# The first block's expert gather turned round: tokens stationary, in f32, with a ninth piece of weights loaded ahead

## What is computed

```python
def expert_choice_ffn(h, w_router, w_gate, w_up, w_down):
    cap = 2 * S // 16                                   # 64 tokens for each of 16 experts
    aff = softmax(h @ w_router)
    gate, idx = top_k(aff.transpose(0, 2, 1), cap)      # each expert chooses its tokens
    xe = h[idx]                                         # the gather: 16 x 64 x 1024
    hid = silu(xe @ w_gate) * (xe @ w_up)               # each weight 1024 x 1024
    ye = (hid @ w_down) * gate
    return zeros.at[idx].add(ye)                        # the scatter
```

## Time and profile before

| | us |
|---|---|
| median of 3 runs | 2611.15 (2604.75 to 2613.42) |
| the profiled execution, its own time | 2608.86 |
| its span in the profile | 2607.0 |
| mean granted TensorE clock | 0.973 of 2.4 GHz |
| PE busy | 2362.6 (91%) |
| DVE busy | 1134.7 (44%) |
| ACT busy | 911.7 (35%) |
| POOL busy | 241.9 (9%) |
| DMA, mean rate over the span | 250 GB/s |

### The profile page before, as it was taken

How to read it: one execution, slowest core, us unless ns; L and a number is a source line. 1 busy time by engine, 2 the same in 40 slices (tenths; PEclk the granted TensorE clock), 3 DMA queues, 4 the chain that set the end, 5 groups by cost and what they waited for, 6 DMA issues and landing times. The chain is left out here.

```text
span 2607.0 us, 31029 instructions
## 1 busy us (share of the span) xinstructions
PE 2362.6 (91%) x12565; PEld 1482.3 (57%) x12565; DVE 1134.7 (44%) x1678; ACT 911.7 (35%) x1228; POOL 241.9 (9%) x114
## 2 busy tenths in 40 slices
PE   6999799888887999799888888999999899989997
PEld 5735533333335835543333328887788777767776
DVE  4984312111214984321112125656612112458997
ACT  3256211111114256211111116656622234247775
POOL 0000100000000000100000005000244322200000
PEclk8999899999998989899999999999999999989999
DMA  9702499999999503399999995423123421149995
GB/s 347 277 1 100 159 388 409 410 410 410 410 408 356 211 0 119 153 409 409 410 410 409 410 405 166 162 81 97 65 85 89 133 76 54 49 159 379 369 372 215
DMA packets 276595, 650.47 MB, mean 250 GB/s; under 512 B 12144, under 2 KB 110718, under 8 KB 276222
## 3 DMA queue, kind: packets, MB, share of 16 engines
q1 hardware_dynamic: 272756, 637.98, 65.1%
q0 software_dynamic: 2592, 7.87, 0.8%
q10 hardware_dynamic: 1130, 2.99, 0.3%
HBM read 641.99 MB, written 8.39 MB: 249 GB/s over the span
## 5 line engine op out<-in xcount | busy, mean ns | idle before, releaser
L837 PE MATMUL ps<-ring,hy 128*64 128x512 f32 x992 | 225.6, 596 | 49.7 <-DMA ring<-in_w_up 32.2
L837 PE MATMUL ps<-ring,scr 128*64 128x512 f32 x992 | 225.2, 596 | 37.3 <-DMA ring<-in_w_up 31.3
L1343 DVE TENSOR_TENSOR scr<-scr,ps 128x512 f32<-128x512 f32 x32 | 22.0, 687 | 541.2 <-PE ps L837 541.2
L864 PE MATMUL ps<-ring,scr 128*64 128x512 f32 x1024 | 227.2, 595 | 4.1 <-ACT scr L1054 2.7
L1609 POOL TENSOR_TENSOR raw_r<-raw,w_high 128x2048 fp32r<-128x2048 f32 (+1 forms) x38 | 164.6, 4342 | 463.5 <-ACT w_high L1876 463.5
L1631 PE MATMUL ps<-x_high,w_high 128*128 128x512 f32 x464 | 187.4, 404 | 7.3 <-DVE y L2272 7.3
L2752 DVE TENSOR_TENSOR ring_r<-ring,ring_high 128x2048 fp32r<-128x2048 f32 x77 | 173.0, 2285 | 28.3 <-ACT ring_high L2629 28.2
L1633 PE MATMUL ps<-x_high,raw_r 128*128 128x512 f32 x464 | 184.5, 398 | 0.0
L837 PEld LDWEIGHTS ps<-ring,hy 128*64 128x64 f32 x992 | 69.2, 137 | 202.3 <-issue 122.4
L1632 PE MATMUL ps<-xT_r,w_high 128*128 128x512 f32 x464 | 183.5, 396 | 0.0
L837 PEld LDWEIGHTS ps<-ring,scr 128*64 128x64 f32 x992 | 68.1, 137 | 188.4 <-issue 121.1
(11 more groups left out here) (581 smaller groups left out, 4520.4 us busy)
## 6 DMA issues: line engine op xcount, KB each, us to landing
ring<-in_w_up SPq DMA_DIRECT2D x64, 2048.0 KB, 23.6
ring<-in_w_down SPq DMA_DIRECT2D x64, 2048.0 KB, 23.5
ring<-in_w_gate SPq DMA_DIRECT2D x60, 2048.0 KB, 23.3
ring<-in_w_up SPq DMA_DIRECT2D x56, 1024.0 KB, 6.9
ring<-in_w_ada SPq DMA_DIRECT2D x22, 2048.0 KB, 13.7
ring<-in_w_down SPq DMA_DIRECT2D x28, 1024.0 KB, 6.6
raw<-in_w_in SPq DMA_DIRECT2D x24, 1024.0 KB, 5.0
raw<-in_w_in SPq DMA_DIRECT2D x20, 512.0 KB, 5.2
```

The costliest lines, as they stand in the source:

```text
L837: mm = pe.matmul(ps[CAP * half:CAP * (half + 1), 1 + j // 2, :], x_e[j % 2][:, at_x:at_x + CAP], weights[:, k, half * HALF:(half + 1) * HA ...
L864: mm = pe.matmul(ps[CAP * half:CAP * (half + 1), 4, :], hidT[:, at_f:at_f + CAP], weights[:, k, half * HALF:(half + 1) * HALF], start=(j = ...
```

## The change

`gather` is turned round: `h_tok` in f32 is the stationary side, in blocks of 128 tokens by 128 channels, and s_pair, now f32, is the moving side with 128 columns. For each of 8 tiles of channels, 4 products add up; the result already stands as channels by slots in PSUM, where DVE's `tokens` reads it. So the eviction to `x_rows`, `turn_tokens`, ACT's rounded copies (line 1039) and POOL's subtractions (line 501) go. The first half of `one_hot_T`, which held the high part, takes (1, 2) as a third early piece, issued with (1, 0). The slots of the ring move by one: the six loads that wait for pieces 1 to 6 are now (1, 3) to (2, 2), and the rule 6e + j - 5 holds from (2, 3) on. Three loads for the next layer (`load_ada`) wait for one more used piece each.

```diff
-    early = [... for x, a in ((hy, CHUNK), (one_hot_T, CHUNK))]
+    early = [... for x, a in ((hy, CHUNK), (one_hot_T, CHUNK), (one_hot_T, 0))]
...
-        slot = (j - 3) % 6
+        slot = (j - 1 - EARLY) % 6
...
-            for e, j in ((0, 0), (0, 4), (0, 5), (1, 0)):
+            for e, j in ((0, 0), (0, 4), (0, 5), (1, 0), (1, 2)):
                 load(e, j)
             for n in range(6):
                 sp.wait_ge(chunk_used, n + 1)
                 load(1 + (n + EARLY) // 6, (n + EARLY) % 6)
...
-                    sp.wait_ge(chunk_used, used - (5 - c))
+                    sp.wait_ge(chunk_used, used - (4 - c))
                     load_ada(sp, A, M, after, c, ahead)
-                sp.wait_ge(xe_mm, 2 * PAIRS)
+                sp.wait_ge(xeT_mm, 2 * PAIRS)
...
-            for i in range(2 * TT):
-                pool.wait_ge(htok_ev, i + 1)
-                cs = slice((i % 2) * HALF, (i % 2 + 1) * HALF)
-                pool.tensor_tensor(h_low3[:, i // 2, cs], h_tok3[:, i // 2, cs], h_high3[:, i // 2, cs].bitcast(F32), ALU.subtract).then_inc(htok_low, 1)
...
             def gather(n):
                 pe.wait_ge(s_built, n + 1)
                 for half in range(2):
-                    cs = slice(half * HALF, (half + 1) * HALF)
-                    for t in range(TT):
-                        pe.matmul(ps[:, GATHER_BANKS[half], :], s_pair[:, t, :], h_high3[:, t, cs], start=(t == 0), stop=False)
-                        mm = pe.matmul(ps[:, GATHER_BANKS[half], :], s_pair[:, t, :], h_low3[:, t, cs], start=False, stop=(t == TT - 1))
-                    mm.then_inc(xe_mm, 1)
-            def turn_tokens(n):
-                for half in range(2):
-                    pe.wait_ge(xe_kept, 2 * n + (half + 1))
                     for b in range(4):
                         kt = 4 * half + b
-                        mm = pe.transpose(ps[:, GATHER_BANKS[half], b * P:(b + 1) * P], x_rows[:, kt * P:(kt + 1) * P], ident)
+                        for t in range(TT):
+                            mm = pe.matmul(ps[:, GATHER_BANKS[half], b * P:(b + 1) * P], h_tok3[:, t, kt * P:(kt + 1) * P], s_pair[:, t, :], start=(t == 0), stop=(t == TT - 1))
                     mm.then_inc(xeT_mm, 1)
...
                     gates(n + 1)
-                    turn_tokens(n + 1)
...
-                act.activation(h_tok3[:, i // 2, cs], ps[:, 2 + i % 4, :], ACT.Copy, scale=factor)
-                act.activation(h_high3[:, i // 2, cs], ps[:, 2 + i % 4, :], ACT.Copy, scale=factor).then_inc(htok_ev, 1)
+                act.activation(h_tok3[:, i // 2, cs], ps[:, 2 + i % 4, :], ACT.Copy, scale=factor).then_inc(htok_ev, 1)
...
-            def gathered(n):
-                for half in range(2):
-                    act.wait_ge(xe_mm, 2 * n + (half + 1))
-                    act.activation(x_rows[:, half * HALF:(half + 1) * HALF], ps[:, GATHER_BANKS[half], :], ACT.Copy).then_inc(xe_kept, 1)
```

More of the change, by code:

```diff
@@ L325, in layer @@
     chunk = [ring[:, i * CHUNK:(i + 1) * CHUNK].rearrange("p (k n) -> p k n", k=4) for i in range(6)]
-    early = [x[:, a:a + CHUNK].rearrange("p (k n) -> p k n", k=4) for x, a in ((hy, CHUNK), (one_hot_T, CHUNK))]
+    early = [x[:, a:a + CHUNK].rearrange("p (k n) -> p k n", k=4) for x, a in ((hy, CHUNK), (one_hot_T, CHUNK), (one_hot_T, 0))]
     EARLY = len(early)
@@ L364, in layer @@
     x_e, sg, hid = (scr[:, 0, :], hy[:, 7 * S:8 * S]), scr[:, 1, :], scr[:, 2, :]
-    x_rows = hy[:, D:2 * D]
     hidT = sg
-    s_pair = M["scr_r"][:, 3, :].rearrange("p (t n) -> p t n", t=TT)
-    h_high3 = M["one_hot_T_r"][:, 0:CHUNK].rearrange("p (t d) -> p t d", t=TT)
-    h_low3 = M["h_tok_r"][:].rearrange("p (t d) -> p t d", t=TT)
+    s_pair = scr[:, 3, :].rearrange("p (t n) -> p t n", t=TT)
     rowsT_done, vec_ready, ada_in = sem("rowsT_done"), sem("vec_ready"), ahead["ada"]
@@ L386, in layer @@
     wout_done, x1_ready = sem("wout_done"), sem("x1_ready")
-    r_mm, rT_kept, r_done, r_sub, r_exp, aff_ready, affT_done, htok_mm, htok_ev, htok_low, rank_ready, rankT_done = (
-        sem(n) for n in ("r_mm", "rT_kept", "r_done", "r_sub", "r_exp", "aff_ready", "affT_done", "htok_mm", "htok_ev", "htok_low", "rank_ready", "rankT_done"))
+    r_mm, rT_kept, r_done, r_sub, r_exp, aff_ready, affT_done, htok_mm, htok_ev, rank_ready, rankT_done = (
+        sem(n) for n in ("r_mm", "rT_kept", "r_done", "r_sub", "r_exp", "aff_ready", "affT_done", "htok_mm", "htok_ev", "rank_ready", "rankT_done"))
     r_bias_mm, r_bias_kept, r_scaled, xe_scaled, sel_built = (sem(n) for n in ("r_bias_mm", "r_bias_kept", "r_scaled", "xe_scaled", "sel_built"))
     chunk_in, early_in = [sem(f"chunk_in{i}") for i in range(6)], [sem(f"early_in{i}") for i in range(EARLY)]
-    xe_kept, xeT_mm = sem("xe_kept"), sem("xeT_mm")
-    chunk_used, s_built, xe_mm, xe_ready, st_mm, st_free, sg_ready, hid_ready, hidT_mm, hidT_ready, ye_free = (
-        sem(n) for n in ("chunk_used", "s_built", "xe_mm", "xe_ready", "st_mm", "st_free", "sg_ready", "hid_ready", "hidT_mm", "hidT_ready", "ye_free"))
+    xeT_mm = sem("xeT_mm")
+    chunk_used, s_built, xe_ready, st_mm, st_free, sg_ready, hid_ready, hidT_mm, hidT_ready, ye_free = (
+        sem(n) for n in ("chunk_used", "s_built", "xe_ready", "st_mm", "st_free", "sg_ready", "hid_ready", "hidT_mm", "hidT_ready", "ye_free"))
     ye_hi_ready, ye_lo_ready, out_done, x2_ready = (sem(n) for n in ("ye_hi_ready", "ye_lo_ready", "out_done", "x2_ready"))
@@ L787, in _ @@
             pe.wait_ge(htok_ev, 2 * TT)
-            pe.wait_ge(htok_low, 2 * TT)
             def gather(n):
@@ L809, in gates @@
                 for t in range(TT):
-                    pe.matmul(ps[:, 7, 0:2], s_pair[:, t, :].bitcast(F32), aff[:, t, bass.ds(2 * n, 2)], start=(t == 0), stop=(t == TT - 1))
+                    pe.matmul(ps[:, 7, 0:2], s_pair[:, t, :], aff[:, t, bass.ds(2 * n, 2)], start=(t == 0), stop=(t == TT - 1))
                 pe.wait_ge(sel_built, n + 1)
@@ L869, in _ @@
             gates(0)
-            turn_tokens(0)
             expert(0, 0, True, False)
@@ L1050, in pair_of_experts @@
                     act.activation(sg, ps[:, 1, :], ACT.Silu).then_inc(sg_ready, 1)
-                    if r == 1 and not last:
-                        gathered(n + 1)
                     act.wait_ge(hidT_mm, 2 * n + (r + 1))
@@ L1067, in pair_of_experts @@
                 act.activation(ye_hi, ye, ACT.Copy).then_inc(ye_hi_ready, 1)
-            gathered(0)
             pair_of_experts(0, True, False)
```

## The result

The changed kernel takes 2615.75 us (median of 20 runs, 2609.32 to 2619.96), the kernel before 2609.44 us (20 runs, 2602.30 to 2615.71): ratio 1.0026, with a 95% interval of 1.0018 to 1.0034. It is 6.3 us slower, about 0.25%. The interval leaves out 1, and the difference is inside the 0.3% that the prediction had set as its border. The forecast was 2616 us, and +6.3.

The account below looks back on a forecast made before the run. The landing of (2, 4), issued once (1, 4) is used, then 79 gapless transfers were taken as the bound; 3.7 us in the first layer plus 2.6 in the second gave +6.3, put down as 2616 us, range 2608 to 2625.

Parts of the forecast that it names:

- The bound: Each layer's end: PE's work up to the use of (1, 4), 7.9 us until (2, 4) lands, then 79 transfers.
- The ninth piece, worth nothing: Loading (1, 2) early gains nothing, because the load that sets the end, (2, 4), depends on PE.
- The forecast stand of 7.5 us: DMA standing idle between the landings of (2, 3) and (2, 4): 12.6 - 5.1 = 7.5 us.
- The gather's price: New gather at full clock: 64 records of 0.113 us, 7.2 us against the old 3.8, 3.4 us more.
- Inside the pair: Second gather: 3.4 us dearer, less 1.0 us of transposes removed, so 2.4 us more of PE for each pair.
- Ahead of the first product: First gather 3.5 us longer, 2.2 us less between it and the first product: first use 1.3 us later.
- the sum of 3.7: First layer's delay: 1.3 us ahead of the first product plus 2.4 us in the second gather.
- The second layer: Its delay: 3.7 us less 1.1 us of slack in the issue of (2, 4), so 2.6 us.
- the slower case: Clock returns only after the first gather, 13.7 us instead of 10.1: +13.5 us in all, 2624 us; chance 0.12.
- Hidden delays: Loads are further ahead than read, so PE's 3.7 us never reach the end: 2611 us; chance 0.09.
- a ninth piece that pays: The stream sets the end, so the extra early piece moves it -3.8 us a layer: about 2603 us; chance 0.10.
- A gather no dearer than the old: New gather takes 3.6 us, shortening PE's chain by 2.3 and 1.2 us: about -8 us, 2602 us; chance 0.04.

Follow-up runs that it names:

- e3: The changed kernel with the gathers of pairs 0 and 1 taking only the first 128 tokens: 2600.72 us, ratio 0.9962 to the kernel before.
- e6: The changed kernel with the second gather and its gates moved behind the products with (1, 4) and (1, 5): 2612.10 us, ratio 1.0015 to the kernel before.
- e1: The changed kernel with eight pieces loaded ahead, (1, 2) back in the ring: 2615.68 us, ratio 1.0029 to the kernel before.
- e4: The changed kernel with eight pieces ahead and the gathers of pairs 0 and 1 taking only 128 tokens: 2603.47 us, ratio 0.9976 to the kernel before.
- e2: The changed kernel with the gathers of pairs 2 to 7 taking only the first 128 tokens: 2620.36 us, ratio 1.0043 to the kernel before.
- e9: The changed kernel with eight pieces ahead and ACT's copies and POOL's subtractions back as dead work: 2615.75 us, ratio 1.0020 to the kernel before.

## Why the prediction was right

**The bound.** Forecast: the use of (1, 4), 7.9 us, and 79 transfers. (2, 4) is issued right behind the use of (1, 4) in the changed kernel too, at 370.37, and lands 7.8 us later. e3 and e6 moved that use, and the end followed PE as long as PE was what lagged ahead of (2, 4).

**The ninth piece, worth nothing.** e1 shows it, to 0.1 us. The forecast stand of 7.5 us ahead of (2, 4) measured 7.6. The reason given, that the end depends on PE, is borne out by e3 and e4: with a shorter PE chain the same piece is worth 1.4 and 4.0 us at (2, 4). The later waits of `load_ada`, put at nothing, are taken back in e1 with no change either.

**The gather's price.** Forecast 7.2 us at full clock; measured 7.25. The same-shaped row of the second block was the right one. By the Trainium skill, "TensorE: Matmul & The Clock Gate", section "Back-to-back issue gap", the 64 records would have been an estimated 3.6 us at 56 ns each and an estimated 5.2 us at the 81 ns that it gives with weight loads. The trace agrees with neither, an f32 record of 128 columns starting every 0.113 us here.

**Inside the pair.** Forecast +2.4 us on PE's chain; measured 49.5 - 47.1 = 2.4, and that only the second gather of the eight pays it is shown by e2.

**Ahead of the first product.** Forecast +1.3 us; measured +0.7 and +1.2. This was a little too much: I gave the new gather the half clock of the old one, 6.05 and 5.0 us, and it had 4.7 in both layers. That is not the new gather's doing: in e1, e2, e6 and e9, which have the same gather, it was 4.7 to 5.3. In the first layer the sum of 3.7 thus became 3.2 at (2, 4)'s issue and 2.9 in the stage.

**The second layer.** Forecast 2.6, from 3.7 and a slack of 1.1; measured 3.5. The slack was there ((2, 4) lands 2.2 us later, counted from the gather, than before), but behind it the stream took 405.7 us instead of 404.4 us: the late landing behind a stand, which the forecast did not have and whose cause stays open. It and the smaller first term cancel: 2.9 + 3.5 = 6.4 instead of 3.7 + 2.6 = 6.3. That the sum is closer than its terms is luck, and so is the agreement of the medians to 0.1 us, since parts that no edit touches can move a median by more (e2).

**The rivals.** The clock came back inside the gather, at 314.7, so the slower case did not happen; e3 shows that a shorter gather does run into it. Hidden delays and a ninth piece that pays are ruled out by e1 and by the stages. A gather no dearer than the old is ruled out by its 7.25 us; that rival's own gains of 2.3 and 1.2 us a layer add up to 7 us, not to the 8 put down.

## What to carry to other kernels

A buffer more is worth something, at most a transfer, only if the last load that is late waits for the DMA; if it waits for a consumer's progress through the ring, the buffer turns into a longer stand, and one look at that load's issue, its landing and the use just before tells which. Of work repeated in a loop beside a saturated stream, only the repeats ahead of the last stand are paid: here two gathers of eight. And before TensorE's first burst after a pause, look at its granted clock: eleven to fourteen idle products in the pause gave back 4.4 us in either kernel, two thirds of the 6.3 us that this change cost, and 22 to 26 of them, which outlasted the pause, cost 13 to 16 us.

## What the runs showed that I had not expected

An f32 product with 128 columns of weights and 512 moving columns takes 0.86 us alone (22.48 us for 26), while of products with 64 columns of weights two run side by side, one per 0.43 us. A short burst may end before the clock is back and leave its half clock to what follows (e3: 5.6 us of products at 0.50). Programs with unchanged instructions ahead of the edit differed by up to 4.9 us before the first gather (308.8 to 313.7 us in the profiles without delaying products), and in e2 this showed as a stretch of 13.7 us at half clock. After the DMA had stood ahead of (2, 4), even for the 0.4 us of the kernel before, one of the next landings was late by another 0.8 to 1.4 us; the cause was not tried.
